# A fused decoder layer: pooled differences shared between VectorE and GpSimd, decode keys issued ahead of the pooled products

## The chip, the cores and the metric

The kernel runs on one core of one Trainium2 chip. A core has a matrix engine (PE, TensorE), a vector engine (DVE), a scalar engine (ACT), GpSimd (POOL) and SyncE (SP), which issues most of the DMAs; each follows its own instruction list and meets the others at semaphores. PE's weight loads are listed apart as PEld. The metric is the device time of one execution in microseconds (us); the figure that counts is the median of several runs. On one core, 0.2% of it (4 us) is about what a measurement can tell from no change.

## What is computed

One layer of a hybrid decoder over 1024 prompt tokens and 8 decode tokens (1032 columns, kept transposed: channels on the partitions, tokens along the free axis), in float32. The parts that the change touches are the causal mean pooling over windows of 2, 4, 8 and 16 tokens, one for each group of 128 channels, and the attention of the 8 decode tokens over their cached memory keys:

```python
def pool_mix(u, buf, pos0, w_pool, pool_scale):
    z = jnp.concatenate([buf, u], axis=1)           # buf: the 15 tokens before
    cs = jnp.concatenate([zeros, jnp.cumsum(z, axis=1)], axis=1)
    for g, w in enumerate((2, 4, 8, 16)):
        hi = cs[:, 16:16 + T, sl]; lo = cs[:, 16 - w:16 - w + T, sl]
        cnt = jnp.minimum(w, pos0 + t + 1)
        means.append((hi - lo) / cnt)
    d = concatenate(means) - u                      # the pooled difference
    y = einsum('btgc,gcd->btgd', d, w_pool) * pool_scale
...
def memory_attention(qx, mk, mv):
    s = einsum('bthd,bmhd->bhtm', qx, mk) * (XATTN_DH ** -0.5)
    return einsum('bhtm,bmhd->bthd', softmax(s), mv)
```

For the prompt the first w-1 tokens have a smaller divisor (1, 2, ... w-1); for each decode token the mean is that of its own value and the last w-1 of its buffer. So d has three kinds of columns: the first w-1 (the edge), the middle, and the last 8 (the decode columns).

## The kernel before

**Stages.** Norms and gates (to about 100 us), four mLSTM heads (each a loop over 8 chunks, to 1005 us), a short stage with the pooling and the decode keys (1005 to 1037 us), the memory attention with the merge of the branches (to 1189), the output product, and the feed-forward (to the end). All dense matmuls go through `product` (L892) as three passes of high and low parts; three groups of 344 columns (`NG`, `tok[g]`) share three PSUM banks. The order of work is written out by hand for each engine, and the waits are on counting semaphores.

**The short stage.** Four engines work on it:

- SP loads `u_pad` (the pool channels), `bufT` (the decode buffers), `wp`, two slabs of merge weights, `xq` (queries) and the keys of the first four decode tokens, `kv_in` and `v_in`; keys 4 to 7 each follow the use of key b-4 (`s_dkeys_used`).
- POOL (L763 to 784) makes the windowed sums by doubling: 1, 2, 3 and 4 additions for windows 2, 4, 8, 16 (`win_a` to `win_e`, L768), each counted on `s_window_step`. Then it splits two slabs of weights into high and low (`head_split`, L702 and L704) and stages the first 128 queries (`xs_t`, L780).
- DVE, behind the last head's additions (L1958), copies the decode queries into `xq_rows` (L1973) and fills `inv_count` (L1976). For each window w it then makes `d = pool_d[:, w % 2]`: the sum over `bufT` (L1994), the difference over all 1032 columns (the helper at L1763), then the decode and edge columns again (L1996 to L1998 and L1763), and gives `s_pool_d_ready`. Between them come the low parts `yp_lo` of the window before (`pool_lo`, the helper L1763 too), which free the PSUM banks. After the windows it makes the decode pool state (L2004, L2005), the maximum and the small softmax of the decode rows (L2009 to L2013, `dec_exp`), `pool_lo(3)` and `dec_probs` (L2016).
- PE alternates, for w = 0 to 3: the keys of two decode tokens (L1083, from `cache_t` or from `P_sb` and `PT_sb`), then the pooled product of window w (L892, `pool_d` by `wp`). After the transposes of `dec_exp` (L1091) the attention's loop begins with L1110, which needs `dec_probs`, the staged queries and, for its first merge group, a split slab.
- ACT takes each pooled product out of PSUM (`pool_hi`, L1420) and makes the exponential of the decode scores (L1427) between `pool_hi(2)` and `pool_hi(3)`.

## Time and profile before

| | us |
|---|---|
| median of 3 runs | 2012.83 (2011.98 to 2015.08) |
| the profiled execution | 2014.58 |
| its span in the trace | 2012.8 |
| busy in it: PE, weight loads | 1957.8, 1908.2 |
| busy in it: DVE, ACT, POOL | 903.7, 621.5, 896.5 |
| first decode key on PE | 1007.02 |
| start of the attention loop on PE (L1110) | 1036.78 |

How to read it: "busy" is the time in which an engine executes; a share of 97% on PE says that the matmuls of the long stages fill the span, and nothing of a short stage in which it waits. The chain of waits goes back from the last instruction to what released it, and so names, at each moment, the one thing that was waited for. A timeline row gives start and duration of an instruction or of several alike (xN), and in brackets how long its engine was idle before it and what ended that. The granted clock is TensorE's, as a share of 2.4 GHz.

### The profile page before, as it was taken

Reading aid. Unit: us, or ns where it says so; the run is one execution under the profiler, and the core shown is the slowest. Engines: PE = TensorE matmul, PEld = TensorE weight load, DVE = VectorE, ACT = ScalarE, POOL = GpSimd, SP = SyncE. Lnnn points to the kernel's source line nnn. Section 1 sums busy time; section 2 is a strip of 40 time slices with the busy share of each in tenths; the row PEclk is TensorE's granted clock in tenths of the full one; section 3 lists DMA queues with packets and bytes.
Section 4 is the critical chain, followed back from the end, with each engine's and each line's share of the span. In section 5 each row is a group of like instructions: output and inputs, shape, how many; then the busy total and the mean of one; then the engine's idle time right before and its main releaser. Section 6 shows DMA issues by size and latency. Waiting matters only on the chain.

```text
span 2012.8 us, 33480 instructions
## 1 busy us (share of the span) xinstructions
PE 1957.8 (97%) x13077; PEld 1908.2 (95%) x13077; DVE 903.7 (45%) x1966; ACT 621.5 (31%) x1184; POOL 896.5 (45%) x533
## 2 busy tenths in 40 slices
PE   8999999999999999999989999799999999999996
PEld 6999999999999999999969999699999999999996
DVE  6504550154403552054577743888676740111126
ACT  6312211122012220122146546644444453212121
POOL 7453233333333233423442237579777764443412
PEclk9999999999999999999999999899999999999999
DMA  5312331134211331123654354513323252223412
GB/s 190 105 43 85 136 110 43 43 115 141 74 53 58 136 136 43 43 89 141 225 175 147 123 158 129 137 46 124 124 88 125 77 211 87 103 85 105 147 53 85
DMA packets 89289, 218.22 MB, mean 108 GB/s; under 512 B 7721, under 2 KB 40745, under 8 KB 88793
## 3 DMA queue, kind: packets, MB, share of 16 engines
q1 hardware_dynamic: 78784, 192.48, 28.6%
q10 hardware_dynamic: 10392, 24.14, 3.4%
q8 instruction: 84, 1.38, 0.3%
q14 instruction: 29, 0.23, 0.0%
HBM read 162.93 MB, written 53.66 MB: 108 GB/s over the span
## 4 chain that ended last, share of the span: by engine, by line
PE 88%; DVE 5%; issue 2%; ACT 2%; POOL 2%; DMA 0%; DVEq 0%; SPq 0%; ACTq 0%; POOLq 0%
PE bank L892 78%; PE bank L1041 1%; PE bank L1044 1%; PE bank L1235 1%; PE bank L1033 1%; PE bank L996 1%; PE bank L1039 1%; PE bank L1133 1%; POOL w_lo L698 1%; DMA w_raw<-w_stream 0%; ACT P_sb L1437 0%; POOL h_lo L713 0%; DVE acc L2074 0%; DVE gates L2071 0%; DVE acc L1763 0%
## 5 line engine op out<-in xcount | busy, mean ns | idle before, releaser
L892 PE MATMUL bank<-h_hi,w_hi 128*128 128x344 f32 (+1 forms) x2048 | 651.1, 318 | 2.4 <-POOL w_lo L698 2.2
L892 PE MATMUL bank<-h_lo,w_hi 128*128 128x344 f32 (+1 forms) x2048 | 637.7, 311 | 0.0
L892 PE MATMUL bank<-h_hi,w_lo 128*128 128x344 f32 (+1 forms) x2048 | 636.0, 311 | 0.0
L702 POOL TENSOR_TENSOR w_hi<-w_raw,ones 128x1024 fp32r<-128x1024 f32 x77 | 147.4, 1914 | 628.1 <-PE bank L892 628.1
L892 PEld LDWEIGHTS bank<-h_hi,w_hi 128*128 128x128 f32 x2048 | 387.4, 189 | 7.1 <-issue 3.5
L892 PEld LDWEIGHTS bank<-h_hi,w_lo 128*128 128x128 f32 x2048 | 387.2, 189 | 0.9
L892 PEld LDWEIGHTS bank<-h_lo,w_hi 128*128 128x128 f32 x2048 | 387.1, 189 | 0.0
L704 POOL TENSOR_TENSOR w_lo<-w_raw,w_hi 128x1024 fp32r<-128x1024 f32 x77 | 185.7, 2412 | 6.1
L2241 DVE TENSOR_TENSOR acc<-acc,bank 128x344 f32<-128x344 f32 x72 | 36.9, 513 | 292.0 <-PE bank L892 292.0
L1268 ACT ACTIVATE side_t<-bank 128x344 f32<-128x344 f32 x96 | 44.0, 459 | 284.3 <-PE bank L892 284.3
L1763 DVE SCALAR_TENSOR_TENSOR acc<-acc,rstd 128x258 f32<-128x258 f32 x128 | 126.7, 1032 | 0.1
L892 PE MATMUL bank<-f_hi,w_hi 128*128 128x344 f32 x384 | 123.1, 320 | 2.0 <-DVE acc L2241 2.0
L892 PE MATMUL bank<-f_lo,w_hi 128*128 128x344 f32 x384 | 122.7, 319 | 0.0
L892 PE MATMUL bank<-f_hi,w_lo 128*128 128x344 f32 x384 | 122.4, 319 | 0.0
L1268 ACT ACTIVATE o_h<-bank 128x344 f32<-128x344 f32 x40 | 18.4, 459 | 234.9 <-PE bank L892 234.8
L859 POOL TENSOR_TENSOR w_lo<-w_lo_raw,w_hi 128x1024 fp32r<-128x1024 f32 x16 | 38.4, 2402 | 97.3 <-ACT w_hi L1675 97.3
L1899 DVE TENSOR_TENSOR SW<-bank,SW 128x128 f32<-128x128 f32 x32 | 9.3, 292 | 159.2 <-ACT SW L1393 159.2
L2152 DVE TENSOR_TENSOR acc<-acc,bank 128x258 f32<-128x258 f32 x96 | 39.7, 423 | 81.5 <-PE bank L892 42.8
L892 PEld LDWEIGHTS bank<-f_hi,w_hi 128*128 128x128 f32 x384 | 72.2, 188 | 2.9 <-DVE acc L2241 1.9
L854 POOL TENSOR_TENSOR f_lo<-f_raw,f_hi 128x1032 fp32r<-128x1032 f32 x28 | 70.6, 2524 | 4.5 <-ACT f_hi L1683 4.5
L892 PEld LDWEIGHTS bank<-f_lo,w_hi 128*128 128x128 f32 x384 | 72.2, 188 | 0.0
L892 PEld LDWEIGHTS bank<-f_hi,w_lo 128*128 128x128 f32 x384 | 72.1, 188 | 0.0
(434 smaller groups left out, 4407.7 us busy)
## 6 DMA issues: line engine op xcount, KB each, us to landing
w_raw<-w_stream SPq DMA_DIRECT2D x113, 512.0 KB, 3.7
d_side<-side_t ACTq DMA_DIRECT2D x32, 516.0 KB, 2.6
f_raw<-d_f SPq DMA_DIRECT2D x24, 516.0 KB, 4.5
gates<-d_side SPq DMA_DIRECT2D x24, 344.0 KB, 4.1
d_f<-sq SPq DMA_DIRECT2D x16, 516.0 KB, 3.3
dC<-stC SPq DMA_DIRECT2D x32, 256.0 KB, 3.7
qkb<-d_qk SPq DMA_DIRECT2D x32, 256.0 KB, 4.0
o_C_s<-dC SPq DMA_DIRECT2D x32, 256.0 KB, 2.0
```

The costliest lines, as they stand in the source:

```text
L698: pool.tensor_tensor(w_lo[:, slot, :], w_raw[:, slot, :], w_hi[:, slot, :].bitcast(F32), ALU.subtract)\
L702: pool.tensor_tensor(w_hi[:, slot, :], w_raw[:, slot, :], ones[:, 0:1].to_broadcast([P, 1024]), ALU.mult).then_inc(s_hi_made, 1)
L704: pool.tensor_tensor(w_lo[:, slot, :], w_raw[:, slot, :], w_hi[:, slot, :].bitcast(F32), ALU.subtract)\
L854: pool.tensor_tensor(f_lo[c % 2][:, k, :], f_raw[c % 2][:, k, :], f_hi[c % 2][:, k, :].bitcast(F32), ALU.subtract).then_inc(s_f_row_lo, 1)
L859: pool.tensor_tensor(w2_lo[u % 4], w2_raw[u % 4], w2_hi[u % 4].bitcast(F32), ALU.subtract)\
L892: last = pe.matmul(out, st, mv, start=i == 0, stop=i == n - 1)
L996: last = pe.transpose(b_tr[r][:, (c % 2) * 256 + k * P:(c % 2) * 256 + (k + 1) * P], src[:, k, c * L:(c + 1) * L], ident[:, :])
L1033: last = pe.matmul(b_S[:, 0:L], ks[:, k, :], qs[:, k, :], start=k == 0, stop=k == 1)
L1268: act.activation(out, bank[g + 3 * second][:, 0:G], func, scale=scale).then_inc(s_group_free[g], 1)
L1763: return dve.scalar_tensor_tensor(out=out, in0=in0, scalar=scalar, in1=in1, op0=op0, op1=op1)
L2152: dve.tensor_tensor(d_t[s], t1[s] if p == 1 else d_t[s], m, ALU.subtract if p == 2 else ALU.add)\
L2241: dve.tensor_tensor(acc[:, u % 8, tok[g]], acc[:, u % 8, tok[g]], bank[g + 3 * second][:, 0:G], ALU.add)\
```

## The change

What it does, part by part:

- **First queries.** The copy into `xq_rows` goes from DVE to ACT, behind ACT's wait for `u_pad`.
- **Differences.** DVE makes all four sums over `bufT` at once into a new tile `held` and fills 16 columns of `inv_count` before them (`s_pool_d_ready` reaches 5). For each window it then makes only the middle columns. GpSimd makes edge and decode columns in a new function `edges(w, steps)`, five small instructions for each window in three steps with waits: `edges(0)` and `edges(1)` after the third addition, behind a wait for `s_pool_d_ready` 5; `edges(2)` and `edges(3)` after the last addition.
- **Weight splits.** The two `head_split` calls go from before the first staging copy `xs_t` to behind it.
- **PE's order.** Keys 0 to 3, product 0, keys 4 and 5, product 1, keys 6 and 7, products 2 and 3. A product waits for `s_pool_d_ready` and for GpSimd's `s_window_step` (6, 9, 19, 22).

```diff
@@ GpSimd
+            def edges(w, steps):
+                win = 2 << w
+                u, d, src = u_pad[:, w, :], pool_d[:, w % 2, :], (win_a, win_c, win_b, win_e)[w]
+                if w >= 2:
+                    pool.wait_ge(s_group_ready[2], UNIT_POOL + w - 1)
+                pool.tensor_tensor(held[:, w, :], held[:, w, :], u[:, 16 + T:16 + N], ALU.add)
+                pool.tensor_tensor(d[:, 0:win - 1], src[:, 16:16 + win - 1], inv_count[:, 0:win - 1], ALU.mult).then_inc(s_window_step, 1)
+                pool.wait_ge(s_window_step, steps + 1)
+                pool.tensor_tensor(held[:, w, :], held[:, w, :], inv_count[:, win - 1:win].to_broadcast([P, ND]), ALU.mult)
+                pool.tensor_tensor(d[:, 0:win - 1], d[:, 0:win - 1], u[:, 16:16 + win - 1], ALU.subtract).then_inc(s_window_step, 1)
+                pool.wait_ge(s_window_step, steps + 2)
+                pool.tensor_tensor(d[:, T:N], held[:, w, :], u[:, 16 + T:16 + N], ALU.subtract).then_inc(s_window_step, 1)
+
             for w, wins in enumerate(((win_a,), (win_b, win_c), (win_b, win_d, win_b), (win_d, win_e, win_d, win_e))):
                 src = u_pad[:, w, :]
+                if w == 2:
+                    pool.wait_ge(s_pool_d_ready, 5)
+                    edges(0, 3)
+                    edges(1, 6)
+                    steps = 9
...
-            for j in range(SLABS_PER_HEAD, SLABS_PER_HEAD + 2):
-                head_split(HEADS - 1, j)
-
+            edges(2, 16)
+            edges(3, 19)
             pool.wait_ge(s_xq_loaded, 64)
             for c in range(NC):
                 if c:
                     pool.wait_ge(s_xbias_ready, c + 1)
                 pool.tensor_copy(xs_t[:, :, :], xq[:, :, c * L:(c + 1) * L]).then_inc(s_xs_staged, 1)
+                if c == 0:
+                    for j in range(SLABS_PER_HEAD, SLABS_PER_HEAD + 2):
+                        head_split(HEADS - 1, j)
@@ TensorE
-                pe.wait_ge(s_pool_d_ready, w + 1)
+            def pool_product(w):
+                pe.wait_ge(s_pool_d_ready, 6 + w)
+                pe.wait_ge(s_window_step, (6, 9, 19, 22)[w])
                 for g in range(NG):
                     group(g, UNIT_POOL + w, [(wp[:, w, :], pool_d[:, w % 2, tok[g]])], False)
@@ ScalarE
             act.dma_start(o_pool, u_pad[:, :, 16 + T - 15:16 + T]).then_inc(s_pool_stored, 16)
+            act.wait_ge(s_set_up, 8)
+            act.wait_ge(s_xq_loaded, 64)
+            act.activation(xq_rows[:, :, :].rearrange("p a b -> p (a b)")[:, 0:1024:33].rearrange("p (h b) -> p h b", h=4),
+                           xq[:, :, T:N], ACT.Copy).then_inc(s_dsoftmax, 1)
@@ VectorE
-            for t in range(15):
-                dve.memset(inv_count[:, t:t + 1], 1.0 / (t + 1))
+            for t in range(16):
+                last = dve.memset(inv_count[:, t:t + 1], 1.0 / (t + 1))
+            last.then_inc(s_pool_d_ready, 1)
...
             for w in range(4):
+                dve.tensor_reduce(held[:, w, :], bufT[:, w, :, 15 - ((2 << w) - 1):15], axis=AX.X, op=ALU.add).then_inc(s_pool_d_ready, 1)
+            for w in range(4):
...
-                held = sm[:, ND * (w % 2):ND * (w % 2 + 1)]
-                dve.tensor_reduce(held, bufT[:, w, :, 15 - (win - 1):15], axis=AX.X, op=ALU.add)
-                step(stt(d, src[:, 16:], 1.0 / win, u[:, 16:], ALU.mult, ALU.subtract))
-                dve.tensor_tensor(held, held, u[:, 16 + T:], ALU.add)
-                step(dve.tensor_tensor(d[:, 0:win - 1], src[:, 16:16 + win - 1], inv_count[:, 0:win - 1], ALU.mult))
-                dve.tensor_tensor(d[:, 0:win - 1], d[:, 0:win - 1], u[:, 16:16 + win - 1], ALU.subtract)
-                stt(d[:, T:N], held, 1.0 / win, u[:, 16 + T:], ALU.mult, ALU.subtract).then_inc(s_pool_d_ready, 1)
+                stt(d[:, win - 1:T], src[:, 16 + win - 1:16 + T], 1.0 / win, u[:, 16 + win - 1:16 + T], ALU.mult, ALU.subtract)\
+                    .then_inc(s_pool_d_ready, 1)
```

**Where it moves instructions.** On GpSimd, from the third addition to the first staging copy, before (`win_*` are the windowed sums, `w_hi` and `w_lo` the split weights, `xs_t` the staged queries):

```order
L768 TENSOR_TENSOR win_c<-win_b 128x1032
L768 TENSOR_TENSOR win_b<-u_pad 128x1032
...
L768 TENSOR_TENSOR win_e<-win_d 128x1032
L702 TENSOR_TENSOR w_hi<-w_raw,ones 128x1024
L704 TENSOR_TENSOR w_lo<-w_raw,w_hi 128x1024
L702 TENSOR_TENSOR w_hi<-w_raw,ones 128x1024
L704 TENSOR_TENSOR w_lo<-w_raw,w_hi 128x1024
L780 COPY xs_t<-xq 128x512 x3
```

And now, the same place, with the first edge block (a second like it follows) and the fourth:

```order
L788 TENSOR_TENSOR win_c<-win_b 128x1032
L772 TENSOR_TENSOR held<-held,u_pad 128x8
L773 TENSOR_TENSOR pool_d<-win_a,inv_count 128x1
L775 TENSOR_TENSOR held<-held,inv_count 128x8
L776 TENSOR_TENSOR pool_d<-pool_d,u_pad 128x1
L778 TENSOR_TENSOR pool_d<-held,u_pad 128x8
...
L788 TENSOR_TENSOR win_e<-win_d 128x1032
...
L778 TENSOR_TENSOR pool_d<-held,u_pad 128x8
L799 COPY xs_t<-xq 128x512
L702 TENSOR_TENSOR w_hi<-w_raw,ones 128x1024
L704 TENSOR_TENSOR w_lo<-w_raw,w_hi 128x1024
```

Twenty small instructions have come in, ten in the middle of the additions and ten behind them, and the splits stand behind the staging copy.

On TensorE, from the end of the last head's products to the attention loop, before (`xq_rows` by a key slab is a decode key, `pool_d` by `wp` a pooled product):

```order
L892 MATMUL bank<-y_lo,w_hi 128x344
L1083 MATMUL bank<-cache_t,xq_rows 32x256 x8
L892 MATMUL bank<-pool_d,wp 128x344 x3
L1083 MATMUL bank<-P_sb,xq_rows 32x256 x4
L1083 MATMUL bank<-PT_sb,xq_rows 32x256 x4
L892 MATMUL bank<-pool_d,wp 128x344 x3
L1083 MATMUL bank<-cache_t,xq_rows 32x256 x8
L892 MATMUL bank<-pool_d,wp 128x344 x3
L1083 MATMUL bank<-P_sb,xq_rows 32x256 x4
L1083 MATMUL bank<-PT_sb,xq_rows 32x256 x4
L892 MATMUL bank<-pool_d,wp 128x344 x3
L1091 MATMUL bank<-ident,dec_exp 128x32 x2
```

And now:

```order
L914 MATMUL bank<-y_lo,w_hi 128x344
L1105 MATMUL bank<-cache_t,xq_rows 32x256 x8
L1105 MATMUL bank<-P_sb,xq_rows 32x256 x4
L1105 MATMUL bank<-PT_sb,xq_rows 32x256 x4
L914 MATMUL bank<-pool_d,wp 128x344 x3
L1105 MATMUL bank<-cache_t,xq_rows 32x256 x8
L914 MATMUL bank<-pool_d,wp 128x344 x3
L1105 MATMUL bank<-P_sb,xq_rows 32x256 x4
L1105 MATMUL bank<-PT_sb,xq_rows 32x256 x4
L914 MATMUL bank<-pool_d,wp 128x344 x6
L1125 MATMUL bank<-ident,dec_exp 128x32 x2
```

Each product but the last stands behind one more pair of keys, and the last two products stand together (x6).

On DVE, behind the last head's additions, before (`sm` holds the sum over `bufT`):

```order
L1958 TENSOR_TENSOR acc<-acc,bank 128x344 x24
L1973 COPY xq_rows<-xq 128x32
L1976 MEMSET inv_count 128x1 x15
L1994 TENSOR_REDUCE sm<-bufT 128x8
L1763 SCALAR_TENSOR_TENSOR pool_d<-win_a,u_pad 128x1032
L1996 TENSOR_TENSOR sm<-sm,u_pad 128x8
L1997 TENSOR_TENSOR pool_d<-win_a,inv_count 128x1
L1998 TENSOR_TENSOR pool_d<-pool_d,u_pad 128x1
L1763 SCALAR_TENSOR_TENSOR pool_d<-sm,u_pad 128x8
```

And now:

```order
L1996 TENSOR_TENSOR acc<-acc,bank 128x344 x24
L2010 MEMSET inv_count 128x1 x16
L2021 TENSOR_REDUCE held<-bufT 128x8 x4
L1801 SCALAR_TENSOR_TENSOR pool_d<-win_a,u_pad 128x1023
L1801 SCALAR_TENSOR_TENSOR pool_d<-win_c,u_pad 128x1021
L1801 SCALAR_TENSOR_TENSOR yp_lo<-bank,vec,yp_hi 128x344 x3
L1801 SCALAR_TENSOR_TENSOR pool_d<-win_b,u_pad 128x1017
```

The fills and the reductions, for which GpSimd now waits, stand directly behind the head's additions, and the small instructions between the differences are gone.

## Rows read from the trace of the kernel before

**Rows 1.** Chain of waits, the pooling stage: start us, us, what.

```profile
1015.05 2.21 DVE sm L1996
...
1029.61 3.58 PE bank L1083 x16
...
1033.22 0.42 DVE sm L2009
```

**Rows 2.** Timeline of PE: start, us, line, instruction [idle before it, releaser].

```profile
1007.02 3.61 PE L1083 MATMUL bank<-cache_t,xq_rows 128*32 128x256 f32 x16 [1.96 <-DVE xq_rows L1973]
1013.84 3.60 PE L892 MATMUL bank<-pool_d,wp 128*128 128x344 f32 x6 [3.20 <-DVE pool_d L1763]
...
1027.64 1.97 PE L892 MATMUL bank<-pool_d,wp 128*128 128x344 f32 x6 [1.12 <-DVE yp_lo L1763]
...
1036.78 1.99 PE L1110 MATMUL bank<-kv_in,xs_t 128*128 128x256 f32 x8 [1.43 <-DVE dec_probs L2016]
```

**Rows 3.** SyncE's issues, and DMAs with us from issue to landing.

```profile
990.78 0.47 SPq L519 DMA_DIRECT2D xq<-d_side  x1
992.49 0.43 SPq L530 DMA_DIRECT2D cache_t<-ckT  x1
...
xq<-d_side SPq DMA_DIRECT2D x1, 516.0 KB, 13.3
cache_t<-ckT SPq DMA_DIRECT2D x1, 512.0 KB, 14.3
PT_sb<-ckT SPq DMA_DIRECT2D x1, 512.0 KB, 15.9
cache_t<-ckT SPq DMA_DIRECT2D x1, 512.0 KB, 4.2
```

**Rows 4.** Timeline of POOL in the pooling stage.

```profile
999.01 1.91 POOL L768 TENSOR_TENSOR win_c<-win_b 128x1032 f32<-128x1032 f32 x1
...
1004.97 1.91 POOL L768 TENSOR_TENSOR win_b<-win_d 128x1032 f32<-128x1032 f32 x1
...
1013.77 3.47 POOL L768 TENSOR_TENSOR win_e<-win_d 128x1032 f32<-128x1032 f32 x1
1017.31 1.89 POOL L702 TENSOR_TENSOR w_hi<-w_raw,ones 128x1024 fp32r<-128x1024 f32 x1
1019.28 2.37 POOL L704 TENSOR_TENSOR w_lo<-w_raw,w_hi 128x1024 fp32r<-128x1024 f32 x1
...
1026.85 0.63 POOL L780 COPY xs_t<-xq 128x512 f32<-128x512 f32 x1
```

**Rows 5.** Timeline of DVE in the pooling stage.

```profile
1005.10 0.51 DVE L1958 TENSOR_TENSOR acc<-acc,bank 128x344 f32<-128x344 f32 x1 [0.43 <-PE bank L892]
1005.53 1.39 DVE L1973 COPY xq_rows<-xq 128x32 f32<-128x32 f32 x1
1006.86 0.24 DVE L1976 MEMSET inv_count<- 128x1 f32 x15
...
1028.38 0.26 DVE L1994 TENSOR_REDUCE sm<-bufT 128x8 f32<-128x120 f32 x1
1028.56 1.22 DVE L1763 SCALAR_TENSOR_TENSOR pool_d<-win_e,u_pad 128x1032 f32<-128x1032 f32 x1
...
1031.72 0.59 DVE L2004 COPY win_a<-bufT 128x112 f32<-128x112 f32 x4
```

**Rows 6.** Windows; the last columns: granted PE clock, DMA share, GB/s.

```profile
1013.80:1017.40 3.60, 3.56 (x7) 1.86 (x8) 3.53 (x5) 1.10 (x2) 3.52 (x2) 0.54 0.12 48
1035.20:1036.80 1.60, 0.17 (x3) 0.07 (x2) 1.34 (x4) 0.50 (x2) 0.00 (x0) 1.00 0.28 40
```

**Rows 7.** Single lines on POOL: duration in ns, min/median/max.

```profile
L817 POOL TENSOR_TENSOR x_in<-x_in,acc x28: 723/744/1724, 1240.6 to 1296.2; 128x258 f32<-128x258 f32 x28
...
L878 POOL TENSOR_TENSOR x_back<-x_back,acc x14: 903/929/936, 1973.2 to 2006.1; 128x344 f32<-128x344 f32 x14
...
L760 POOL MEMSET win_a<- x1: 108/108/108, 986.1 to 986.1; 128x16 f32 x1
```

## What the change was predicted to do

> **What bounds the kernel now.** I read three views, in this order: the chain of waits over the stretch between the last head and the memory attention (1005 to 1037 us), the timelines of PE, DVE and POOL over the same stretch, and the granted clock there. Over the rest of the span the matmuls of L892 are the chain, and nothing in them changes. The change lives in some 32 us of 2012.8, so its worth is read there.
>
> In that stretch no single engine is the bound. PE begins the first decode keys at 1007.02, is idle 3.20 us before the first pooled product and 1.12 us before the third, and begins the attention (L1110) at 1036.78 [rows 2]. Its own work there is four pairs of keys of 3.6 us and four pooled products of 1.97 us: 22.3 us of the 29.8. DVE makes the differences, and waits in the middle of small instructions: an addition of 8 elements takes 2.21 us because a GpSimd addition is under way [rows 1, 4]; the copy of 32 elements into xq_rows takes 1.39 us, from 1005.53 until GpSimd's win_b ends at 1006.88 [rows 4, 5]. GpSimd loses as well: win_e takes 3.47 us where win_c takes 1.91 [rows 4]. So a DVE instruction whose operands all lie in SBUF and a GpSimd instruction do not run together here. The chain ends in the last keys (1029.61 to 1033.19), then the maximum at 1033.22 and the small softmax of the decode rows up to L1110, 3.56 us later [rows 1, 2].
>
> **First queries on ScalarE, and two keys ahead.** The copy of xq_rows leaves DVE. Its input is issued at 990.78 and lands 13.3 us later, at 1004.1 [rows 3]; ScalarE is idle, so the copy is done before PE comes. But the second key slab is issued at 992.49 and takes 14.3 us: 1006.8 [rows 3]. The first keys start at about 1006.9 rather than 1007.02: gain 0.1 us. The second pair of keys needs a slab issued two behind that one (an issue takes 0.4 to 0.5 us, so at about 993.5), and it takes 15.9 us [rows 3]: 1009.4, before PE asks at 1010.5. Keys 4 to 7 are issued by SyncE as the earlier ones are used (from 1008.9 on) and land 4.2 us later [rows 3], at 1015 for the third pair, wanted at 1016. PE: 1006.9 + 3.6 + 3.6 = 1014.1, product 0 (its inputs are ready by then, next part) to 1016.1, keys to 1019.7, product 1 to 1021.7, last keys to 1025.3. That is 7.9 us earlier than 1033.2, and both idle gaps are gone up to there. What is then late is products 2 and 3.
>
> **GpSimd's new path.** It does ten additions of 1.91 us, 1.98 with the step between them [rows 4]. Before, they ran from 995.0 to 1017.2 without a wait. Now the fourth waits until DVE has made inv_count and the four sums over bufT, and DVE does that only behind its last addition of the head at 1005.10 + 0.51 [rows 5]. Sixteen fills (0.24 us for fifteen) and four reductions (0.26 for the longest, [rows 5]) make it 1006.4. GpSimd has stood still since win_c ended at 1000.92 [rows 4]: **5.5 us lost**, with seven additions still to make.
>
> From 1006.4: DVE's differences for windows 0 and 1 want the same port and cost 1.22 us each [rows 5]: 2.4. Then two edge blocks. A block is five additions or products of 1 to 15 elements in three steps. No row shows one so small. Additions of 258 elements take 0.744 us and of 344 0.929 [rows 7]: 2.15 ns an element, so 0.21 us at 8 elements. The ends are 0.11 us (a fill of 16 elements) and 0.72 us (the fastest of 258 elements, as if all of it were fixed) [rows 7]. I take 0.21, as the slope fits two rows of the same instruction. Three steps of 0.21 + 0.08, and 0.1 for each of the two that run right behind another, make a block 1.1 us (ends 0.7 and 3.8). Two blocks: 1011.0. Three additions for window 2: 1017.0. Four for window 3, and DVE's difference for window 2 among them: 7.9 + 1.2, 1026.1. The third block, with the last difference beside it: 1.1 + 1.2, **1028.4**. Product 2 waits for this. It started at 1027.64 [rows 2]: it comes 0.8 us later, not 5 earlier. The fourth block ends at 1029.5; product 3 waits rather for the banks.
>
> The Trainium skill ("GPSIMD Engine Reference", section 3, Performance versus the Vector engine) gives 4497 ns for an addition of 2048 elements at 2.6 cycles an element. An estimate from that page leaves 0.06 us fixed and 0.08 for 8 elements; a block would be near 0.6 us and product 2 at about 1027.0.
>
> **From product 2 to the attention.** PE is done with the keys at 1025.3 and idle for 3.1 us. After an idle time of 3.20 us product 0 took 3.60 us instead of 1.97, at a granted clock of 0.54 of full speed (the 1.2 GHz level) [rows 2, 6]. I take the same here. Then the three takes by ScalarE and DVE are over 4.7 us after its start (3.64 to the third take of product 0, two of about 0.5 behind it), at full clock 3.1: 1033.1, or 1031.5. DVE's five copies for the pool state (0.7 us) stand between that and the maximum [rows 5]; from there to L1110 it is the old 3.56: 1037.4, or 1035.8.
>
> **The splits moved behind.** The two weight splits (1.89 + 2.37 us each, [rows 4]) stood before the first staging copy at 1026.85. Now they run behind it: from 1030.2 to about 1039, which is all of the softmax chain. Their cover is gone in one place: GpSimd was idle from 1027.5 to 1039.7, and DVE's copies and the product on dec_exp (SBUF to SBUF) ran free. Now each may wait for the split under way, 0 to 2.4 us. With the starts above: the copies wait from 1033.1 to 1034.5, and the product on dec_exp 0.5 us. That is **+1.9 us**: L1110 at 1039.3 at the low clock, about 1037.4 at the full one. The first slab is split by 1034.6, before the merge wants it at 1041; the second staging copy comes at 1040, wanted at 1045; SyncE's slab loads and attention_gates behind the splits shift by 1 to 2 us and are wanted later still. These I cost at nothing.
>
> The Trainium skill ("SBUF — State Buffer", section SBUF: two separate sides) calls the shared port pair an exclusive lock held for the full instruction, the loser blocked fully. It speaks against this move, and the 1.39 and 2.21 us above agree. If the port were shared in parts, the 1.9 us would be near nothing.
>
> **Sum.** L1110 at 1039.3 against 1036.78: +2.5 us. The profiled execution took 2014.58 us around a span of 2012.8, so it would take 2017.1; the median of the runs, 2012.83, goes to **2015.3**.
>
> **The rivals.**
> - *The clock stays up and the blocks are cheap.* Blocks at 0.7 us put product 2 at 1027.2, 1.9 us after the keys, too short by the gap of 1.96 us before the first keys, which left the clock up. Then L1110 is at 1035.5 to 1036.8: 0 to 1.3 us faster, 2011.5 to 2012.8. For it: the fills of 0.11 us [rows 7]. Against it: 5.5 us of GpSimd standing still.
> - *The port doesn't bind, and the gain comes.* If the copies and the small softmax slip between GpSimd's instructions and product 2 starts at 1026, L1110 comes at 1033 or before: 4 us faster or a little more, 2008.8. It needs both; [rows 1, 5] speak against it.
> - *Slower by more than 4 us.* GpSimd's small instructions cost more. Fifteen of them stand before product 2, so each 0.1 us more adds 1.5 us. From 0.31 us each upward the total passes +4 us; at 0.72 it is +10 us (2023). A second mechanism with the same sign: product 3 ends by 1034, and PE then has only two small transposes until L1110, so the clock may be low as the attention starts, which adds up to 1.8 us (half speed for a stretch like the 3.6 us of [rows 6]). Before, the gap there was 1.6 us and the clock stayed at 1.00 [rows 6]. The forecast holds neither.
> - *The order changes but the time doesn't*, since the chain only moves from PE to GpSimd: within 1 us, inside "same".
>
> **How the numbers follow.** The likeliest case, product 2 at the low clock and the port waits: 0.45, own range 2013.5 to 2016.5. Clock up, cheap blocks: 0.23. Port doesn't bind: 0.05. Dearer small instructions, or a low clock at the attention on top: 0.27, of it 0.04 beyond +6 us. The range takes all but the last of these and part of the third: 2010.8 to 2019.0. Faster or slower by over 0.2% means by 4.0 us, about what a measurement can tell: faster 0.05, within 0.68, slower 0.27.
>
> **What the profile would show.** The fourth addition on POOL at about 1011, with idle time before it released by a DVE reduction; product 2 at 1028.4, last keys over at 1025.3; the clock in product 2; edge instructions at 0.2 us; DVE's copies and the product on dec_exp at over 1 us; L1110 at 1039.3. Wrong: edge instructions of 0.4 us or more (then it is slower), POOL not waiting at 1001 (then 5 us faster), or the copies at 0.6 us in all (then about 2014).

## The result: slower by 6 us, and the profile after

The changed kernel took 2019.42 us (median of 8 executions, 2016.23 to 2021.62), the kernel before, beside it, 2013.11 us (8 executions, 2011.85 to 2015.08). The ratio is 1.0029, with a 95% interval of 1.0018 to 1.004: by the ratio 5.8 us more, by the medians 6.3. That is 0.29% slower, more than the 0.2% that a measurement can tell, though the interval's lower end, 0.18%, is just under it. The prediction held "within 0.2%" the likeliest and gave 0.27 to slower. Its +2.5 us had the sign and less than half of the size, and the median stands 0.4 us above the upper end of its range, 2019.0; counted by the ratio from the 2012.83 us that the forecast set out from, it is 2018.7, just inside. The profiled execution took 2019.79 us around a span of 2018.0, against 2014.58 and 2012.8.

All times below that are "behind the head" count from the end of the last product of the head on PE: 1004.09 us in the trace of after, 1005.06 in that of before. So the two traces can be laid on each other.

PE's timeline in the pooling stage, after (start, us, instruction, idle time before it with its releaser):

```profile
1005.71 3.61 PE L1105 MATMUL bank<-cache_t,xq_rows 128*32 128x256 f32 x16 [1.62 <-DMA cache_t<-ckT]
...
1012.70 2.00 PE L914 MATMUL bank<-pool_d,wp 128*128 128x344 f32 x6
1014.63 3.64 PE L1105 MATMUL bank<-cache_t,xq_rows 128*32 128x256 f32 x16
...
1026.75 6.76 PE L914 MATMUL bank<-pool_d,wp 128*128 128x344 f32 x12 [2.98 <-issue]
1038.69 0.42 PE L1125 MATMUL bank<-ident,dec_exp 32*128 32x32 f32 x2 [5.18 <-DVE dec_exp L2045]
1040.45 3.77 PE L1144 MATMUL bank<-kv_in,xs_t 128*128 128x256 f32 x8 [1.34 <-DVE dec_probs L2048]
```

It answers [rows 2]. The first keys come 1.6 us behind the head and wait for a DMA now, not for DVE's copy. Product 0 (L914, 1012.70) follows the second keys without a gap, in 2.00 us where it took 3.60. Then come the two idle times that matter: 2.98 us ahead of product 2, and 5.18 us ahead of the transposes (L1125). Products 2 and 3 stand in one row, x12 in 6.76 us, where product 0 is x6 in 2.00. The attention starts at 1040.45, 36.36 us behind the head (before: 31.72), and its first piece takes 3.77 us where it took 1.99.

Line by line for the tile that the pool state leaves by, after: durations in ns, shortest, median, longest, then the first and the last start.

```profile
L2036 DVE COPY win_a<-bufT x4: 205/1456/2368, 1031.6 to 1034.5; 128x112 f32<-128x112 f32 x4
```

The timelines of DVE and of POOL over the same time:

```profile
1031.64 5.25 DVE L2036 COPY win_a<-bufT 128x112 f32<-128x112 f32 x4
1036.81 0.18 DVE L2037 COPY win_a<-u_pad 128x32 f32<-128x32 f32 x1
1036.90 0.40 DVE L2041 TENSOR_REDUCE sm<-bank 32x1 f32<-32x256 f32 x1
...
1038.29 0.34 DVE L2045 TENSOR_SCALAR dec_exp<-dec_exp,sm 32x256 f32<-32x256 f32 x1
```

```profile
1030.20 2.35 POOL L704 TENSOR_TENSOR w_lo<-w_raw,w_hi 128x1024 fp32r<-128x1024 f32 x1
1032.51 1.89 POOL L702 TENSOR_TENSOR w_hi<-w_raw,ones 128x1024 fp32r<-128x1024 f32 x1
1034.48 2.34 POOL L704 TENSOR_TENSOR w_lo<-w_raw,w_hi 128x1024 fp32r<-128x1024 f32 x1
```

This is the heart of the case. Four copies of some 0.2 us each, which took 0.59 together before [rows 5], take 5.25. They begin at 1031.64, inside the first w_lo. The last begins at 1034.5, with the second w_lo, and takes 2.37 us, to the end of that instruction at 1036.82. Between them the whole of w_hi goes by. One by one the four take 0.98, 1.93, 0.21 and 2.37 us. So the copies don't wait once for GpSimd: the first waits for the rest of one of its instructions, the second for the whole of the next, the third slips through, and the fourth waits for the whole of the one after that. The maximum (L2041) stands behind them on DVE and comes at 1036.90. By then the splits are over: the fifth copy goes free, in 0.18 us, and the product on dec_exp takes its old 0.34 us.

The granted clock, after (columns as in [rows 6]: the stretch; busy time of PE, PEld, DVE, ACT and POOL; clock; DMA share; GB/s):

```profile
1026.80:1033.50 6.70, 6.70 (x12) 3.79 (x12) 3.50 (x5) 1.64 (x3) 6.46 (x9) 0.54 0.00 0
1037.00:1046.00 9.00, 5.97 (x17) 5.12 (x18) 4.07 (x11) 3.94 (x9) 0.61 (x1) 0.50 0.71 244
```

and the same stretch of the attention's start in the kernel before:

```profile
1036.80:1046.00 9.20, 9.20 (x61) 8.97 (x61) 4.51 (x12) 7.07 (x15) 0.61 (x1) 1.00 0.82 308
```

After the idle time of 2.98 us products 2 and 3 ran at the 1.2 GHz level (0.5 of full speed), and after that of 5.18 us the transposes and the start of the attention did. Before, the attention began at 1.00.

**Where the 6 us are.** The second attention product, the next one that the trace shows well, stands 51.20 us behind the head, against 43.65: +7.5, of which 4.6 were there at the first one and 2.9 came from the low clock. The first product of z after the attention stands 182.5 us behind the head against 176.6: +5.9. The 1.6 us between come from the clock as well. The trace of before has a stretch at the low clock in the fifth chunk of the attention (that chunk takes 13.8 us where its neighbours take 11.8 to 12.1), and that of after has none:

```profile
1095.00:1099.00 4.00, 4.00 (x22) 3.91 (x22) 2.60 (x7) 0.73 (x3) 0.00 (x0) 0.58 0.55 137
```

(before)

```profile
1094.00:1098.00 4.00, 4.00 (x28) 4.00 (x27) 1.93 (x5) 2.16 (x9) 0.61 (x1) 1.00 0.98 335
```

(after). Behind that product the two traces differ by 0.3 us. The span as a whole grew by 5.2 us, as the head ended 0.97 us sooner in this trace.

### The profile page after: what moved, and what is told of

Same layout as the page of the kernel before. It is cut to its first block, busy times and chain, and to the rows that moved or that the text cites. A ratio compares the mean times of both kernels' runs of the same rounds, so it can differ in the third digit from the quotient of the medians.

```text
span 2018.0 us, 33486 instructions
## 1 busy us (share of the span) xinstructions
PE 1959.5 (97%) x13077; PEld 1909.0 (95%) x13077; DVE 895.4 (44%) x1950; ACT 621.0 (31%) x1185; POOL 900.7 (45%) x553
## 4 chain that ended last, share of the span: by engine, by line
PE 88%; DVE 5%; issue 2%; ACT 2%; POOL 2%; DMA 0%; DVEq 0%; ACTq 0%; POOLq 0%
PE bank L914 78%; PE bank L1063 1%; PE bank L1066 1%; PE bank L1269 1%; PE bank L1055 1%; PE bank L1018 1%; PE bank L1061 1%; POOL w_lo L698 1%; ACT P_sb L1475 0%; POOL h_lo L713 0%; PE bank L952 0%; PE bank L1167 0%; DVE acc L2106 0%; DVE gates L2103 0%; DVE acc L1801 0%
## 5 line engine op out<-in xcount | busy, mean ns | idle before, releaser
L914 PE MATMUL bank<-h_hi,w_hi 128*128 128x344 f32 (+1 forms) x2048 | 650.4, 318 | 2.3 <-POOL w_lo L698 2.1
L914 PE MATMUL bank<-h_lo,w_hi 128*128 128x344 f32 (+1 forms) x2048 | 637.1, 311 | 0.0
L914 PE MATMUL bank<-h_hi,w_lo 128*128 128x344 f32 (+1 forms) x2048 | 635.3, 310 | 0.0
L914 PEld LDWEIGHTS bank<-h_hi,w_hi 128*128 128x128 f32 x2048 | 386.8, 189 | 7.0 <-issue 3.5
L914 PEld LDWEIGHTS bank<-h_hi,w_lo 128*128 128x128 f32 x2048 | 386.6, 189 | 0.9
L914 PEld LDWEIGHTS bank<-h_lo,w_hi 128*128 128x128 f32 x2048 | 386.6, 189 | 0.0
L914 PE MATMUL bank<-f_hi,w_hi 128*128 128x344 f32 x384 | 123.1, 320 | 2.0 <-DVE acc L2273 2.0
L914 PE MATMUL bank<-f_lo,w_hi 128*128 128x344 f32 x384 | 122.7, 319 | 0.0
L914 PE MATMUL bank<-f_hi,w_lo 128*128 128x344 f32 x384 | 122.4, 319 | 0.0
L914 PEld LDWEIGHTS bank<-f_hi,w_hi 128*128 128x128 f32 x384 | 72.2, 188 | 2.9 <-DVE acc L2273 1.9
L914 PEld LDWEIGHTS bank<-f_lo,w_hi 128*128 128x128 f32 x384 | 72.2, 188 | 0.0
L914 PEld LDWEIGHTS bank<-f_hi,w_lo 128*128 128x128 f32 x384 | 72.1, 188 | 0.0
```

Source lines behind the costliest of these rows:

```text
L914: last = pe.matmul(out, st, mv, start=i == 0, stop=i == n - 1)
```

## The experiments

The theory after the result: the loss is DVE's copies waiting for GpSimd's splits, several times over, and the low clock that the long idle time of PE brings. The rivals: GpSimd's later start (5.5 us of standing still) sets the end; or the low clock alone does; or the new order on PE itself costs something. Each kernel is compared with runs of the kernel before on the same chip. The table gives all eleven; "first" and "second" are the starts of the first and second attention product behind the head, "us" is what the first piece took in the same form of row as above. The last three columns come from one profiled execution each, which in e3, e5, e6, e8 and e9 was the slowest of its kernel; the medians come from 8 to 10 executions.

| kernel | median us | before beside it | ratio (95%) | first | us | second |
|---|---|---|---|---|---|---|
| before | 2013.11 | | | 31.72 | 1.99 | 43.65 |
| after | 2019.42 | 2013.11 | 1.0029 (1.0018 to 1.004) | 36.36 | 3.77 | 51.20 |
| e1_split_waits | 2013.23 | 2013.24 | 1.0 (0.999 to 1.001) | 31.39 | 2.69 | 45.15 |
| e2_edges_later | 2012.37 | 2013.24 | 1.0002 (0.9992 to 1.0012) | 30.78 | 3.78 | 44.60 |
| e3_copies_early | 2013.20 | 2013.24 | 0.9999 (0.9989 to 1.0009) | 30.49 | 3.77 | 45.19 |
| e4_filler | 2017.31 | 2013.24 | 1.0024 (1.0013 to 1.0034) | 34.71 | 1.99 | 46.66 |
| e5_all_three | 2008.86 | 2012.5 | 0.9979 (0.997 to 0.9989) | 26.39 | 3.55 | 39.90 |
| e6_edges_copies | 2007.97 | 2012.5 | 0.9978 (0.9967 to 0.9988) | 29.33 | 3.62 | 42.95 |
| e7_before_pe_order | 2012.72 | 2012.5 | 0.9999 (0.9989 to 1.0009) | 29.13 | 3.78 | 43.99 |
| e8_before_split_over | 2017.43 | 2012.5 | 1.0026 (1.0016 to 1.0035) | 35.55 | 3.66 | 49.16 |
| e9_best_filler | 2007.93 | 2013.08 | 0.997 (0.996 to 0.998) | 27.59 | 1.99 | 39.54 |
| e10_pe_order_filler | 2013.08 | 2013.08 | 1.0001 (0.9992 to 1.0011) | 30.83 | 1.89 | 42.69 |
| e11_one_copy | 2016.62 | 2013.08 | 1.0018 (1.0009 to 1.0028) | 34.86 | 3.77 | 48.84 |

**The port wait taken away, by holding the splits back.** GpSimd's splits wait until the small softmax is through.

```diff
 (head's last splits, behind the first staging copy)
+                    pool.wait_ge(s_dsoftmax, 3)
```

> The changed kernel, with GpSimd's two weight splits held back until DVE has made the last product of the small softmax (a wait for s_dsoftmax 3), so that no GpSimd instruction runs beside DVE's pool-state copies. Port theory (the copies of L2036 take 5.25 us in the changed kernel because three split instructions run between them; alone they take 0.6): the copies take 0.6 us, the first attention product (L1144) starts 4.5 us earlier, counted from the last head product on PE: 32 us behind it instead of 36.3; if the clock stays up over the shorter gap, another 2 to 3 us; median 2012 to 2015. Rival (the time is lost earlier, by the late product 2 alone, and the copies' length is hidden): L1144 stays at 36 us and the median near 2019. Second rival (the splits then come too late for the merge): the merge groups wait for the slab, and half of the gain is gone.

The copies are back at 0.59 us, and the loss is gone, as expected: 2013.23 us, ratio 1.0. The first attention product comes 5.0 us sooner than in after (31.39 against 36.36). Timelines of DVE, POOL and PE:

```profile
1031.33 0.59 DVE L2037 COPY win_a<-bufT 128x112 f32<-128x112 f32 x4
```

```profile
1033.73 1.89 POOL L702 TENSOR_TENSOR w_hi<-w_raw,ones 128x1024 fp32r<-128x1024 f32 x1 [5.47 <-DVE dec_exp L2046]
```

```profile
1035.46 2.69 PE L1145 MATMUL bank<-kv_in,xs_t 128*128 128x256 f32 x8 [1.45 <-DVE dec_probs L2049]
```

GpSimd's stall behind the head (5.80 us) is still in this kernel, so by itself it does not make the kernel slower than before. The splits now begin at 1033.73 and end some 8.6 us later (two of 1.89 and 2.35 us, as above), and the median is the old one: costing their later end at nothing was right.

**The edge blocks later on GpSimd.** Windows 0 and 1 get their edges behind the three additions of window 2, so GpSimd does not stand still behind the head.

```diff
-                if w == 2:
+                if w == 3:
...
-                    edges(0, 3)
-                    edges(1, 6)
-                    steps = 9
+                    edges(0, 6)
+                    edges(1, 9)
+                    steps = 12
...
-                pe.wait_ge(s_window_step, (6, 9, 19, 22)[w])
+                pe.wait_ge(s_window_step, (9, 12, 19, 22)[w])
...
-                dve.wait_ge(s_window_step, (1, 3, 12, 16)[w])
+                dve.wait_ge(s_window_step, (1, 3, 6, 16)[w])
```

> The changed kernel, with the wait for DVE and the first two edge blocks moved from in front of window 2's three additions to behind them, so that GpSimd doesn't stand still for 5.5 us. Stall theory: GpSimd's additions end 4 to 5 us earlier, product 2 follows the last keys with no idle time and at full clock, and it is over 6 us earlier; but the splits move forward with them and still lie on DVE's copies, so L1144 starts some 5 us earlier (31 us behind the last head product), and the clock at the attention stays low; median 2014 to 2015. Rival (the port waits alone set the end, the copies end when the splits end): the splits end 5 us earlier too, which gives the same 5 us; told apart by the copies, which by the stall theory still take several us and by a third account (waits only for the instruction under way) at most 3. If neither the stall nor the splits matter: 2019.

Product 2 starts 19.24 us behind the head (after: 22.66) and runs at full clock, in 2.00 us. The first attention product is 5.6 us sooner than in after. The median, 2012.37, is 1.6 us below what was expected, though product 2 gained 3.4 us and not 6. The copies lose nearly as much as before the edit:

```profile
1024.90 4.84 DVE L2036 COPY win_a<-bufT 128x112 f32<-128x112 f32 x4
```

In the trace 3.4 us from product 2's start, 1.8 from its clock (3.11 us from its start to the copies, where after has 4.89) and 0.4 from the copies make the 5.6. The port's 5 us in e1 are another way back to the same time. So the loss has two parts of about equal size, the stall with its low clock and the port waits, and a gain from the rest of the change hides either one: with one part taken away the kernel is as fast as before (e1, e2), with both away it is faster (e5, e6 below). The forecast had priced the first part in full and 1.9 us of the second.

**The copies early.** DVE makes the pool state behind its second difference, when GpSimd is between two additions, and not ahead of the maximum.

```diff
+                if w == 1:
+                    dve.wait_ge(s_pool_d_ready, 6)
+                    dve.wait_ge(s_window_step, 6)
+                    po = win_a[:, 0:480].rearrange("p (k b j) -> p k b j", k=4, b=ND)
+                    for k in range(4):
+                        dve.tensor_copy(po[:, k, :, 0:14], bufT[:, k, :, 1:15])
+                    dve.tensor_copy(po[:, :, :, 14], u_pad[:, :, 16 + T:16 + N]).then_inc(s_pool_state_ready, 1)
...
-            po = win_a[:, 0:480].rearrange("p (k b j) -> p k b j", k=4, b=ND)
-            for k in range(4):
-                dve.tensor_copy(po[:, k, :, 0:14], bufT[:, k, :, 1:15])
-            dve.tensor_copy(po[:, :, :, 14], u_pad[:, :, 16 + T:16 + N]).then_inc(s_pool_state_ready, 1)
```

> The changed kernel, with DVE's five pool-state copies moved from between the low parts of window 2 and the softmax maximum to behind DVE's second difference, where DVE is idle for 6.5 us. Port theory: the maximum follows the low parts at once; what is left on the chain that may wait for a split is the product on dec_exp, at most 2.4 us. L1144 4 to 5 us earlier (31.5 to 32.5 us behind the last head product), median 2013 to 2015. Rival (the small softmax waits for GpSimd as much as the copies did): the product on dec_exp takes 2 us and more, gain 2 to 3 us, 2016 to 2017.

2013.20 us, ratio 0.9999. The first attention product is 5.9 us sooner than in after in the traces, but 1.8 of that are not the edit's doing: in this execution the first keys ran at the low clock (5.30 us in place of 3.61), so the last keys ended later, PE was idle for only 1.06 us ahead of product 2, and that ran at full clock. The splits still run over the small softmax and take 1.1 us from the product on dec_exp. DVE's timeline:

```profile
1031.72 0.14 DVE L2045 TENSOR_SCALAR sm<-sm 32x1 f32<-32x1 f32 x1
1032.48 0.15 DVE L2047 RECIPROCAL sm<-sm 32x1 f32<-32x1 f32 x1 [0.62 <-ACT dec_exp L1465]
1032.67 1.46 DVE L2048 TENSOR_SCALAR dec_exp<-dec_exp,sm 32x256 f32<-32x256 f32 x1
```

and POOL's:

```profile
1031.65 2.35 POOL L704 TENSOR_TENSOR w_lo<-w_raw,w_hi 128x1024 fp32r<-128x1024 f32 x1
```

That is the size at which the prediction put the port: one wait of 0 to 2.4 us. A chain with one such instruction in it loses one wait; of the five copies in after, three lost one each. The two rows of one element per partition run free inside the same w_lo.

**The port wait alone, on the kernel before.** Of the change only this: the splits move behind the first staging copy. So that they fall on the copies as in after, they are also held until product 2 is done.

```diff
-            for j in range(SLABS_PER_HEAD, SLABS_PER_HEAD + 2):
-                head_split(HEADS - 1, j)
-
...
+                if c == 0:
+                    pool.wait_ge(s_group_ready[2], UNIT_POOL + 3)
+                    for j in range(SLABS_PER_HEAD, SLABS_PER_HEAD + 2):
+                        head_split(HEADS - 1, j)
```

> The kernel before with one cost added: the two weight splits are moved behind the first staging copy and held until pooled product 2 is done, so that they run beside DVE's copies and the small softmax, as in the changed kernel; nothing else differs. Port theory: DVE's four copies take 2 to 5 us instead of 0.6, the product on dec_exp may wait too, the first attention product is 3 to 5 us later (35 to 37 us behind the last head product), the clock is low there, and the median is 2017 to 2019: the whole loss of the change, without its other parts. Rival (the loss comes from the new instructions on GpSimd and the stall, and DVE's copies are covered): 2013 to 2014.

2017.43 us, ratio 1.0026: this one part brings 4.9 us of loss to a kernel that has none of the others, where the whole change lost 5.8 to 6.3. Tile row and DVE's timeline:

```profile
L2005 DVE COPY win_a<-bufT x4: 204/1434/2376, 1030.4 to 1033.7; 128x112 f32<-128x112 f32 x4
```

```profile
1030.42 5.21 DVE L2005 COPY win_a<-bufT 128x112 f32<-128x112 f32 x4
...
1037.03 1.09 DVE L2014 TENSOR_SCALAR dec_exp<-dec_exp,sm 32x256 f32<-32x256 f32 x1
```

It also starts the attention at the low clock (3.66 us), after an idle time of PE of 3.37 us ahead of the transposes. At the first attention product 3.8 us are lost, at the second 5.5.

**One copy in place of four.** If every DVE instruction can lose the port anew, fewer instructions lose less.

```diff
-            for k in range(4):
-                dve.tensor_copy(po[:, k, :, 0:14], bufT[:, k, :, 1:15])
+            dve.tensor_copy(po[:, :, :, 0:14], bufT[:, :, :, 1:15])
```

> The changed kernel with DVE's four copies of the decode buffers (one for each channel group) written as one instruction of the same size; it is followed by the copy of the new tokens as before. If a DVE instruction waits at most for the one GpSimd instruction under way when it comes, and the next GpSimd instruction goes first when DVE's next one isn't yet under way, then four copies can meet up to four GpSimd instructions and one copy meets one: the copies' total falls from 5.25 to 0.6 to 3 us, the first attention product is 2.5 to 4.5 us earlier (32 to 34 us behind the last head product), median 2014.5 to 2017. Rival (DVE is kept out until GpSimd's queue of splits is empty): the copy still ends with the last split, 5 us, median 2019.

```profile
1029.97 1.17 DVE L2035 COPY win_a<-bufT 128x448 f32<-128x448 f32 x1
1031.07 1.88 DVE L2036 COPY win_a<-u_pad 128x32 f32<-128x32 f32 x1
...
1034.24 1.22 DVE L2044 TENSOR_SCALAR dec_exp<-dec_exp,sm 32x256 f32<-32x256 f32 x1
```

The copies of the pool state take 2.98 us (1029.97 to 1032.95) in place of 5.35 (1031.64 to 1036.99). The same elements, moved in two instructions and not five, win 2.4 us there, and of the two one still waits for nearly all of w_hi, 1.88 us for 32 elements. The small softmax gives 0.9 back, since it now falls beside the last w_lo. The first attention product is 1.5 us sooner than in after, and the median, 2016.62, is 2.8 below that of after (beside kernels before of 2013.08 and 2013.11); by the ratios, 1.0018 and 1.0029, it is 2.2, and their intervals overlap. The rival, a copy that ends only with the last split, falls in the trace: the copy of 448 elements ended at 1031.14, the last split at 1035.31.

**PE kept busy up to the attention.** After, with 14 products more behind product 3 whose results nobody reads.

```diff
             pool_product(3)
+            for _ in range(14):
+                pe.matmul(b_W[:, 0:MEM], ones[:, :], kv_in[:, 0, :], start=True, stop=True)
             pe.wait_ge(s_dsoftmax, 3)
```

> The changed kernel, with 14 extra products of ones by kv_in on TensorE behind pooled product 3, into a PSUM bank that the attention overwrites; they add work and nothing else, in the 5 us in which TensorE waits for the small softmax. Clock theory (the granted clock is 0.50 from the gap to the middle of the first attention chunk, and L1144 takes 3.77 us instead of 1.99): the clock is 1.00 at L1144, which takes 2.0 us, and the second L1144 starts 3 us earlier; L1144's own start stays at 36 us behind the last head product; median 2016 to 2017. Rival (the low clock is hidden behind the softmax chain of the first chunk, which DVE and ScalarE set): second L1144 within 1 us, median 2019.

The attention starts at full clock:

```profile
1027.16 1.97 PE L914 MATMUL bank<-pool_d,wp 128*128 128x344 f32 x6 [2.01 <-issue]
...
1031.13 6.21 PE L1124 MATMUL bank<-kv_in,ones 128*128 128x256 f32 x28
1037.44 0.31 PE L1127 MATMUL bank<-ident,dec_exp 32*128 32x32 f32 x2
```

2017.31 us against 2019.42 are 2.1 us less by the medians, 1.0 by the ratios (1.0024 and 1.0029, with overlapping intervals). So 1 to 2 us of the loss are the low clock, and the runs bear out little more than the sign. The trace shows more: the second attention product comes 4.5 us sooner than in after. Of this 1.7 is there at the first one and is not the filler's doing, since product 2 found a gap of 2.01 us here, not 2.98, and the clock had stayed up. The other 2.9 are the clock at the attention's start, and part of them is given back: a chunk later in the loop takes 13.6 us, in a stretch at the low clock that after doesn't have. The copies still take 4.63 us, and 4 us of loss stay. So the low clock alone is not the cause, and that rival falls.

**The new order on PE alone, on the kernel before.** Two keys ahead of the products, and the first queries copied by ScalarE; POOL and DVE as before.

```diff
-            for w in range(4):
+            def dec_keys(w):
...
+            def pool_product(w):
...
+            dec_keys(0)
+            dec_keys(1)
+            pool_product(0)
+            dec_keys(2)
+            pool_product(1)
+            dec_keys(3)
+            pool_product(2)
+            pool_product(3)
...
+            act.wait_ge(s_set_up, 8)
+            act.wait_ge(s_xq_loaded, 64)
+            act.activation(xq_rows[:, :, :].rearrange("p a b -> p (a b)")[:, 0:1024:33].rearrange("p (h b) -> p h b", h=4),
+                           xq[:, :, T:N], ACT.Copy).then_inc(s_dsoftmax, 1)
...
-            dve.tensor_copy(xq_rows[:, :, :].rearrange("p a b -> p (a b)")[:, 0:1024:33].rearrange("p (h b) -> p h b", h=4),
-                            xq[:, :, T:N]).then_inc(s_dsoftmax, 1)
```

> The kernel before with only two parts of the change: the first queries copied by ScalarE, and TensorE's new order of keys and pooled products; edge and decode columns stay on DVE, and the splits where they were. If TensorE's order is worth something by itself, the idle time before product 0 goes (3.2 us) and with it the low clock in it (1.6 us); but DVE's windows still wait for GpSimd's additions inside their small instructions, so that product 3 waits for DVE at about 1029.5 and the end of the last keys no longer sets the end; the small softmax then starts behind DVE's copies at 1032.4 instead of 1033.2: first attention product 0.8 to 3 us earlier than before (29 to 31 us behind the last head product), median 2010.5 to 2012.5. Rival (TensorE's order is worth nothing without GpSimd's part, DVE's chain sets the end as before): within 0.5 us, 2013.

The good part of the change is real and worth nothing by itself: the first attention product comes 2.6 us sooner (29.13 against 31.72), and 2012.72 us is the old time. PE's timeline:

```profile
1028.37 3.01 PE L892 MATMUL bank<-pool_d,wp 128*128 128x344 f32 x6 [2.31 <-DVE yp_lo L1778]
1031.48 0.42 PE L1102 MATMUL bank<-ident,dec_exp 32*128 32x32 f32 x2
1033.24 3.78 PE L1121 MATMUL bank<-kv_in,xs_t 128*128 128x256 f32 x8 [1.34 <-DVE dec_probs L2027]
```

The keys had been PE's work between and behind the late products. Without them it idles, and the attention starts at the low clock: the second product stands at 43.99, where it stood at 43.65. In the traces, what the order wins up to the first attention product is gone at the second, where the low clock lies between. The median, 2012.72, is just above the 2010.5 to 2012.5 expected.

**The edits together.** All three (e5: splits held, edges later, copies early), and two of them (e6: edges later, copies early; splits not held). The diffs are those above; only the copies wait for window step 9, as the edges have moved.

> The changed kernel with the three edits of the first runs together: the first two edge blocks behind window 2's additions, DVE's pool-state copies where DVE is idle, and the splits held back until the small softmax is over. If the losses are separate and add up (the stall, the port waits of the copies, the port wait on dec_exp), the low parts of window 2 end some 22.5 us behind the last head product as in the second run, and the first attention product starts 3.6 us later: 26 us behind the last head product, against 31.7 in the kernel before; the median 2007 to 2009, 5 us faster than before. Rival (the splits then bind: 4.3 us from the end of the small softmax to the first split slab, while the merge groups want it after 3.8 us or less): first attention product at 26 us, but the second only 3 to 4 us earlier than before, median 2009 to 2011. Second rival (each edit already gives all there is to gain, the end is set elsewhere): 2013.

> As the run before it, without holding the splits back: they run behind the staging copy, over the small softmax, where now only the product on dec_exp can wait for one. Port theory: that product takes 0.34 to 2.4 us instead of 0.34, and the first attention product is 0 to 2 us later than with the splits held back (26 to 28 us behind the last head product), but the first slab is split long before the merge; median 2008 to 2010. Rival (the whole small softmax is slowed by splits): over 2 us later, 2011 and more.

2008.86 and 2007.97 us, ratios 0.9979 and 0.9978: both faster than before. Holding the splits adds nothing once the copies are out of their way. In e6 the product on dec_exp takes 1.06 us beside a split, in e5 0.34, and the medians don't tell them apart. The profiled execution of e6 was its slowest, 2013.81 us, so its starts in the table stand for that one execution and not for the median. Its first keys came 0.7 us later behind the head than in after, on their DMA, and ran at the low clock:

```profile
1007.79 5.24 PE L1105 MATMUL bank<-cache_t,xq_rows 128*32 128x256 f32 x16 [2.33 <-DMA cache_t<-ckT]
```

**The best version.** e6, and three small products on either side of the transposes (each twice in the records) so that PE is not idle as the attention starts.

```diff
+            pe.wait_ge(s_kv_loaded, 32)
+            def filler(n):
+                for _ in range(n):
+                    pe.matmul(b_W[:, 0:MEM], ones[:, :], kv_in[:, 0, :], start=True, stop=True)
+            filler(3)
             pe.wait_ge(s_dsoftmax, 3)
...
+            filler(3)
             pe.wait_ge(s_dsoftmax, 5)
```

> The changed kernel with the first two edge blocks behind window 2's additions and the pool-state copies moved (the sixth run), and in addition three extra products of ones by kv_in on TensorE behind pooled product 3 and three behind the two transposes, 1.3 us each, into a bank that the attention overwrites: they add work only. Clock theory: the sixth run's first attention product took 3.62 us at the low clock; now it takes 1.99 us, and the second one starts 1.5 to 2.5 us earlier (about 41 us behind the last head product, start of the first unchanged); median 2006 against 2008. Rival (the low clock only fills time that the softmax chain of the first chunk leaves idle): the second starts within 0.5 us, median 2008.

```profile
1029.94 0.31 PE L1130 MATMUL bank<-ident,dec_exp 32*128 32x32 f32 x2 [0.21 <-DVE dec_exp L2054]
1030.18 1.56 PE L1126 MATMUL bank<-kv_in,ones 128*128 128x256 f32 x6
1031.70 1.99 PE L1150 MATMUL bank<-kv_in,xs_t 128*128 128x256 f32 x8
```

2007.93 us, ratio 0.997 (0.996 to 0.998), 5.2 us below the kernel before beside it; the change as it was made stood 6.3 above its own. The attention starts at full clock, 4.1 us sooner than before. Against e6 the median shows no gain (2007.93 and 2007.97, where 2006 was expected); by the ratios, 0.997 and 0.9978, it would be 1.6 us, within the intervals. In the trace a stretch at the low clock turns up in the fifth chunk instead, as in the kernel before.

```profile
1090.00:1094.00 4.00, 4.00 (x21) 3.93 (x22) 2.51 (x7) 0.66 (x3) 0.00 (x0) 0.57 0.51 137
```

**The same filler on the kernel before with the new PE order.** The fillers of e9 in the kernel of e7.

```diff
 (the kernel of e7)
+            pe.wait_ge(s_kv_loaded, 32)
...
+            filler(3)
             pe.wait_ge(s_dsoftmax, 3)
...
+            filler(3)
             pe.wait_ge(s_dsoftmax, 5)
```

> The kernel before with ScalarE's query copy and TensorE's new order (the seventh run, whose first attention product started 2.6 us earlier than in the kernel before, while the median did not move), and in addition the same six extra products. Clock theory (those 2.6 us were given back because the work moved forward leaves TensorE idle before the attention, so that it begins at the low clock): the first attention product takes 1.99 instead of 3.78 us, the second starts 2 us earlier than in the seventh run (42 us behind the last head product), median 2010 to 2011. Rival (the 2.6 us are lost later, in the loop or the merge, whatever the clock): 2012.5 to 2013.

```profile
1028.09 2.85 PE L892 MATMUL bank<-pool_d,wp 128*128 128x344 f32 x6 [2.31 <-DVE yp_lo L1784]
1030.74 2.31 PE L1103 MATMUL bank<-kv_in,ones 128*128 128x256 f32 x6
1032.98 0.30 PE L1107 MATMUL bank<-ident,dec_exp 32*128 32x32 f32 x2
```

The fillers bring nothing here: 2013.08 us, ratio 1.0001, as the rival had it. The clock fell within product 3 (1.00 from 1028.1 to 1029.0, 0.50 from 1029.1), so the first three fillers ran slowly, 2.31 us where those of e9 took 1.46, and the transposes stood behind them. The first attention product comes 1.7 us later than in e7. It then runs in 1.89 us, and the second one is 1.3 us ahead of e7's and 1.0 ahead of before's. Up to the first z product this trace is 2.3 us ahead of before's, but behind it 2.0 us longer (833.2 us to the end of the span, against 831.1), with a stretch at 0.50 from 1336.3 to 1339.6 where before is at 1.00 (1337.5 to 1341.0). The traces of e5, e6 and e8 have such a stretch too, and take 832.2 to 833.2 us there; the other nine have none and take 830.7 to 831.6. Why it comes in some executions, no run here shows.

## Why the prediction was half right

**Each step against the trace.** The terms of the sum, from the end of the head to the attention's first product:

| term | predicted us | after us | before us |
|---|---|---|---|
| head to product 2 | 23.3 | 22.66 | 22.58 |
| product 2 to the copies | 4.7 | 4.89 | |
| the five copies | 2.1 | 5.26 | 0.7 |
| maximum to L1144 | 4.1 | 3.55 | 3.56 |
| attention starts behind the head | 34.2 | 36.36 | 31.72 |
| second attention product, beyond that | not in the sum | 14.84 | 11.93 |

- *Keys ahead.* Right. The first keys 1.62 us behind the head, the product 0 gap gone, the last keys over at 19.7 us behind the head (predicted 20.2).
- *GpSimd stands still for 5.5 us.* Right to the tenth: 5.51 us, released by DVE's reduction, as the last column says. The small additions took 0.20 us at 0.21 predicted, so the row at the slope of [rows 7] was the right neighbour. The first block ran beside DVE's two differences and its first two instructions took 1.05 and 1.16 us:

```profile
1005.48 1.05 POOL L772 TENSOR_TENSOR held<-held,u_pad 128x8 f32<-128x8 f32 x1 [5.51 <-DVE held L2021]
1006.49 1.16 POOL L773 TENSOR_TENSOR pool_d<-win_a,inv_count 128x1 f32<-128x1 f32 x1
1007.73 0.20 POOL L775 TENSOR_TENSOR held<-held,inv_count 128x8 f32<-128x8 f32 x1
...
1009.34 1.91 POOL L788 TENSOR_TENSOR win_b<-u_pad 128x1032 f32<-128x1032 f32 x1
```

  The estimate from the Trainium skill ("GPSIMD Engine Reference", section 3, Performance versus the Vector engine) was 0.08 us at 8 elements. The trace doesn't bear that out: 0.20, and at a distance of 0.16 where two follow each other without a step.
- *Product 2.* 22.66 us behind the head against 23.3. The blocks took 1.0 us each where DVE left them alone (1.1 predicted), and the two differences held GpSimd for 1.8 us, not 2.4: 0.85 in the one row and 0.96 in the other beyond 0.20. The chain of waits puts 1.04 us down to "issue" ahead of it (1025.71 to 1026.75). It is GpSimd's third block, whose last row begins at 1026.45: product 2 waits for two things, DVE's difference and the edges, and the view followed the first.

```profile
1024.49 1.22 DVE pool_d L1801
1025.71 1.04 issue
1026.75 3.79 PE bank L914 x6
```

```profile
1026.45 0.20 POOL L778 TENSOR_TENSOR pool_d<-held,u_pad 128x8 f32<-128x8 f32 x1
```

- *Low clock in product 2.* Right, after an idle time of 2.98 us, and product 3 had it too, which the text did not say. It costs the path nothing more: the maximum waits for the copies, not for product 3.
- *The splits over the softmax chain: the step that failed.* "The copies wait from 1033.1 to 1034.5, and the product on dec_exp 0.5 us": +1.9 in all. Measured: +4.6 for the copies, nothing for the product. The mechanism was named rightly; its size was taken as one wait for the instruction under way. Five instructions behind each other wanted the port, GpSimd's next instruction stood ready behind each of its own, and three of the five waited. e8 shows 4.9 us of loss from this alone (with the low clock that it brings at the attention), e1 and e3 take the loss away by taking the copies' waits away, and e11 wins 2.4 us on the copies by making them two.
- *Low clock at the attention: a term left out of the sum.* It stood among the rivals at "up to 1.8 us" and "the forecast holds neither". It came, and it was likely to: by the forecast's own starts PE would be without work from 1034 to 1039, longer than the 3.1 us that it took for product 2's low clock (though the length of an idle time alone does not settle it, see the last section). The start at the low clock costs 2.9 us up to the second attention product in this trace. Behind the loop 1.3 is left of it, as the later stretch of before is missing; between e4 and after it is 2.1 by the medians and 1.0 by the ratios.

The prediction's own sum with these put right: +2.5, less 0.7 for product 2, 3.2 more for the copies, 0.5 less for the product on dec_exp, 0.2 more ahead of the copies, is +4.7, or +4.6 before rounding, at the first attention product, which is what the traces show. With the clock's 1.3 it is +5.9, and measured were +5.8 by the ratio and +6.3 by the medians.

**The rivals.** Of the third, slower by more than 4 us, the sign and the second mechanism held, not the first: the small instructions cost what the forecast said. That the stated range reaches as far up as the measured time is in part luck: it had been drawn that wide for dear small instructions, which did not come, as much as for the low clock, and not for several waits at the port. "The clock stays up and the blocks are cheap" did not happen in the profiled execution, but was near. In e4, where the work ahead of product 2 is that of after, the gap was 2.01 us and the clock stayed up; and still it lost, since the port came behind. Its first keys had come 1.0 us later, so this gap was shorter by chance. "The port doesn't bind" was the other way round.

The Trainium skill ("SBUF — State Buffer", section SBUF: two separate sides) says of the pair that DVE and GpSimd share that whoever comes first has it for the whole instruction and the other blocks fully. The trace agrees for each instruction that waited: 2368 ns for a copy beside a w_lo of 2.34 us. Of DVE's instructions it names as holders those in a mode that uses two ports, and those with two inputs in SBUF. e3's rows fit that in part, in that the RECIPROCAL and the one-element TENSOR_SCALAR went through in 0.14 us beside a split while the TENSOR_SCALAR of 256 elements waited. Which mode each was in, no run here shows.

**Left open.** Why the medians of e7 and e10 are those of before, though the first z product stands 1.0 and 2.3 us further on in their traces. In e10's trace the 2.0 us lost behind it are nearly all of that; and before was profiled in an execution of 2014.58 us, 1.5 above its median, so a median execution of it may lack the stretch at the low clock in the fifth chunk. That was not tested. Whether the later low stretch in the loop hangs on how the attention starts: the nine traces in which it starts at the low clock, or falls to it in the first piece, have no such stretch, and of the four that start at full clock, before, e4 and e9 have one, but e10 has none. A cause was not tested. And why e6's one profiled execution stands 5.8 us above its median: some 2.3 us are its first keys, some 1 the stretch behind the attention (see e10), the rest is not explained. That it is a port for which the copies wait is the name that this text gives it: the runs show that a copy which meets a GpSimd instruction ends with it, and not what lies between the two.

## What to carry to other kernels

Count instructions, not microseconds, where DVE and GpSimd work on SBUF at the same time: each short DVE instruction on the path can wait for one whole GpSimd instruction, so several copies beside long splits are several waits that may come, not one (three of five came here). Before work is moved into an engine's idle time, look who used the port then, and move short copies out from in front of what the path wants. And where work is pulled ahead on PE, sum up what idle time it leaves behind: a low clock that may follow it at the start of the next stage belongs in the sum as a term, not among the rivals.

## What the hardware showed beyond that

- Between two DVE copies that follow each other at once, with no wait between them, GpSimd can come in with its next instruction: four copies 205 to 2368 ns (after), 204 to 2376 (e8), and 210 to 216 when GpSimd is idle (e1). It does not each time: in both runs one of the four went free (205 and 204 ns) between two that waited.

```profile
L2037 DVE COPY win_a<-bufT x4: 210/215/216, 1031.3 to 1031.7; 128x112 f32<-128x112 f32 x4
```

- The length of one idle time of PE does not tell whether the clock falls. Ahead of product 2, 2.01 us left it at 1.00 and 2.98 us went over into 0.54 (e4 and after). But ahead of the first keys 2.59 us left it at 1.00 (e4: 3.61 us), while 1.92 and 2.33 us were followed by 0.50 (e3 and e6: 5.30 and 5.24 us). In e7 the clock fell within product 3, which took 3.01 us behind 2.31 idle.
- The low clock at the attention's start outlasts it: in after the granted clock is 0.50 from 1037 to 1046, though PE has work at every moment from 1040.45 on.
- GpSimd's small additions cost 0.20 us at 1 element as at 8 (L776 and L775), so what is paid at that size is the instruction.
